# Router logits with the router weights stationary in four column groups, their partial sums copied, turned and added by one more product

## What is computed

```
h = h + merged @ w_out
xt = rms_norm(h, norm_ffn_gain)                       # 512 tokens x 1024
logits = xt.astype(f32) @ w_router.astype(f32) + b_router   # 512 x 32
top_val, top_idx = lax.top_k(logits, 4)
gates = softmax(top_val)
# each token's row goes to its 4 experts:
#   g, u = xblk @ w_up_gate[e] + b_up_gate[e];  act = swiglu(g, u);  y = act @ w_down[e] + b_down[e]
# and comes back as the sum of the 4 results, weighted with the gates
```

## Time and profile before

| | |
|---|---|
| median of 3 runs | 1762.51 us (1762.42 to 1762.52) |
| the profiled execution's own time | 1762.06 us |
| its span | 1760.2 us |
| ScalarE (ACT) busy | 1141.1 us, 65% |
| VectorE (DVE) busy | 1420.5 us, 81% |
| GpSimd (POOL) busy | 316.9 us, 18% |
| products of the logits (line 870), 64 records | 7.6 us busy |
| granted TensorE clock, mean | 0.998 |

### The profile page before, as it was taken

One profiled execution on the slowest core, in us unless ns is written; L12 is line 12 of the kernel. 1 busy time (PEld: TensorE's weight loads), 2 busy tenths in 40 slices (PEclk: granted clock), 3 DMA queues, 4 the chain that ended last, 5 costly groups with the idle time before them and its releaser, 6 DMA issues.

```text
span 1760.2 us, 26321 instructions
## 1 busy us (share of the span) xinstructions
PE 1736.3 (99%) x8957; PEld 1281.8 (73%) x8957; DVE 1420.5 (81%) x1450; ACT 1141.1 (65%) x1122; POOL 316.9 (18%) x241
## 2 busy tenths in 40 slices
PE   8999999999999999999999999999999999999997
PEld 7778777777877767777777777777777777777765
DVE  4666576567656899989888988898889888988898
ACT  4544564455454577777777777777777777777783
POOL 1102201210220111122111111121112111211153
PEclk9999999999999999999999999999999999999999
DMA  7432233133126599999999999999999999999995
GB/s 211 144 97 65 79 107 107 36 107 101 43 97 248 199 353 377 359 367 388 378 374 372 356 374 381 362 372 363 379 369 366 366 375 372 369 367 372 380 333 235
DMA packets 159059, 488.44 MB, mean 277 GB/s; under 512 B 13187, under 2 KB 83123, under 8 KB 125521
## 3 DMA queue, kind: packets, MB, share of 16 engines
q1 hardware_dynamic: 151120, 469.29, 72.6%
q0 software_dynamic: 7088, 16.52, 2.8%
q10 hardware_dynamic: 816, 2.19, 0.3%
HBM read 479.43 MB, written 24.39 MB: 286 GB/s over the span
## 4 chain that ended last, share of the span: by engine, by line
PE 96%; DVE 2%; issue 1%; ACT 0%; DMA 0%; DVEq 0%; SPq 0%; ACTq 0%
PE psum L330 28%; PE psum L332 28%; PE psum L331 28%; PE psum L987 1%; PE psum L700 1%; PE psum L730 1%; PE psum L1023 1%; PE psum L971 1%; PE psum L716 1%; PE psum L666 1%; PE psum L683 1%; DVE wL L1735 1%; PE psum L764 0%; PE psum L897 0%; PE psum L675 0%
## 5 line engine op out<-in xcount | busy, mean ns | idle before, releaser
L1735 DVE TENSOR_TENSOR wL<-wraw,wH 128x2048 fp32r<-128x2048 f32 x388 | 882.1, 2289 | 118.5 <-ACT wH L429 115.9
L429 ACT ACTIVATE wH<-wraw 128x2048 fp32r<-128x2048 f32 x388 | 744.3, 1919 | 289.5 <-PE psum L332 280.8
L330 PE MATMUL psum<-wH,xTH 128*96 128x512 f32 x1040 | 416.2, 400 | 0.5 <-DVE wL L1735 0.4
L332 PE MATMUL psum<-wH,xTL 128*96 128x512 f32 x1040 | 408.4, 393 | 0.0
L331 PE MATMUL psum<-wL,xTH 128*96 128x512 f32 x1040 | 408.2, 392 | 0.0
L330 PEld LDWEIGHTS psum<-wH,xTH 128*96 128x96 f32 x1040 | 167.9, 161 | 72.3 <-DVE wL L1735 0.8
L332 PEld LDWEIGHTS psum<-wH,xTL 128*96 128x96 f32 x1040 | 167.8, 161 | 72.4
L331 PEld LDWEIGHTS psum<-wL,xTH 128*96 128x96 f32 x1040 | 168.0, 162 | 69.3
L330 PE MATMUL psum<-wH,aTH 128*96 128x512 f32 x496 | 196.4, 396 | 0.0
L332 PE MATMUL psum<-wH,aTL 128*96 128x512 f32 x496 | 194.9, 393 | 0.0
L331 PE MATMUL psum<-wL,aTH 128*96 128x512 f32 x496 | 194.4, 392 | 0.0
(11 more groups left out here) (272 smaller groups left out, 2161.8 us busy)
## 6 DMA issues: line engine op xcount, KB each, us to landing
wraw<-in_w_up_gate SPq DMA_DIRECT2D x256, 1024.0 KB, 7.0
wraw<-in_w_down SPq DMA_DIRECT2D x128, 1024.0 KB, 7.6
fraw<-in_w_in SPq DMA_DIRECT2D x68, 512.0 KB, 4.1
yd<-in_consts SPq DMA_DIRECT2D x8, 1024.0 KB, 8.2
wraw<-yd SPq DMA_DIRECT2D x3, 2048.0 KB, 11.4
wraw<-in_w_out SPq DMA_DIRECT2D x4, 1024.0 KB, 5.2
xt<-in_x SPq DMA_DIRECT2D x4, 512.0 KB, 5.0
hres<-in_x SPq DMA_DIRECT2D x4, 512.0 KB, 5.1
```

What stands on the lines that cost most here:

```text
L330: nc.tensor.matmul(ps, lh, rh, start=start, stop=False)
L332: return nc.tensor.matmul(ps, ll, rh, start=False, stop=stop)
L429: nc.scalar.activation(wH[:, b % SPLIT, :], raw(b), ACT.Copy).then_inc(p_hi, 1)
L1735: V.tensor_tensor(wL[:, b % SPLIT, :], raw(b), wH[:, b % SPLIT, :].bitcast(F32), ALU.subtract).then_inc(p_lo, 1)
```

## The change

The router block `wr[:, k, :]` (128 x 32) becomes the stationary operand, in one of four groups of 32 columns, and the 128 tokens of `rT` move. Four partial sums, one for each k modulo 4, come out turned, in partitions 32 g to 32 g + 31 of bank 2, columns 128 to 255. ScalarE copies these 128 x 128 numbers into the new tile `lgT` (`logits_turned`), and one more product with `lgT` stationary and a constant of 128 x 32 moving (a one wherever the row modulo 32 is the column) turns and adds them (`logit_sums`). `lg_done` now counts both steps. The lists of TensorE and ScalarE are changed to place the new steps. ROWS_TURNED and LOGITS_TURNED hold the counts of `rT_ready`, which now counts the new copies too.

```
+    lgT = sb("lgT", [P, P])
...
+    ROWS_TURNED, LOGITS_TURNED = ((1, 2), (3, 4), (6, 7), (10, 11)), (5, 8, 9, 12)
...
-            def out_projection(j, q):
+            def out_projection(j, q, halves=(0, 1)):
...
-                for kk in range(2):
+                for kk in halves:
...
-                if j == NT - 1:
+                if j == NT - 1 and halves[-1] == 1:
                     last.then_inc(p_used, 1)
-                elif q == 3:
+                elif q == 3 and halves[-1] == 1:
                     last.then_inc(wo_done, 1)
...
             def logits(j):
 
-                pe.wait_ge(rT_ready, 2 * j + 2)
+                pe.wait_ge(rT_ready, ROWS_TURNED[j][1])
                 pe.wait_ge(tri_wr_ready, 2)
                 pe.wait_ge(h_ready, 4)
                 if j:
                     pe.wait_ge(top_ready, j)
                 for k in range(KD):
-                    last = nc.tensor.matmul(bank[2][:, 0:NE], rT[:, k, j * P:(j + 1) * P], wr[:, k, :],
-                                            start=k == 0, stop=k == KD - 1)
+                    g = slice(k % 4 * NE, (k % 4 + 1) * NE)
+                    last = nc.tensor.matmul(bank[2][g, P:2 * P], wr[:, k, :], rT[:, k, j * P:(j + 1) * P],
+                                            start=k < 4, stop=k >= 4, skip_group_check=True)
                 last.then_inc(lg_done, 1)
+
+            def logit_sums(j):
+
+                pe.wait_ge(rT_ready, LOGITS_TURNED[j])
+                nc.tensor.matmul(bank[2][:, 0:NE], lgT[:, :], cst[:, K_SE:K_SE + NE], start=True, stop=True).then_inc(lg_done, 1)
...
             out_projection(3, 0)
             logits(0)
             turn_rows(2)
+            logit_sums(0)
             out_projection(3, 1)
             logits(1)
             positions(0)
-            out_projection(3, 2)
+            out_projection(3, 2, (0,))
+            logit_sums(1)
+            out_projection(3, 2, (1,))
             logits(2)
             positions(1)
-            out_projection(3, 3)
+            out_projection(3, 3, (0,))
+            logit_sums(2)
+            out_projection(3, 3, (1,))
             first_rows(0)
             turn_rows(3)
             positions(2)
+            logits(3)
             first_rows(1)
-            logits(3)
+            logit_sums(3)
             first_rows(2)
...
+            def logits_turned(j):
+                act.wait_ge(lg_done, 2 * j + 1)
+                A(lgT[:, :], bank[2][:, P:2 * P], ACT.Copy).then_inc(rT_ready, 1)
+
...
             rows_turned(1)
             row_squares(2)
             row_sqrt(2)
+            logits_turned(0)
+            rows_turned(2)
             rows_out(0)
             rows_out(1)
-            rows_turned(2)
-            for b in (4, 5, 6):
-                high(act, 0, b)
+            logits_turned(1)
+            high(act, 0, 4)
+            logits_turned(2)
+            high(act, 0, 5)
+            high(act, 0, 6)
             rows_out(2)
             row_squares(3)
             act.wait_ge(p_used, 4)
             rows_turned(3)
             row_sqrt(3)
+            logits_turned(3)
...
             def route(j):
 
-                dve.wait_ge(lg_done, j + 1)
+                dve.wait_ge(lg_done, 2 * j + 2)
```

More of the change, by code:

```diff
@@ L856, in turn_rows @@
                     if j:
-                        pe.wait_ge(rT_ready, 2 * (j - 1) + half + 1)
+                        pe.wait_ge(rT_ready, ROWS_TURNED[j - 1][half])
                     for k in range(4 * half, 4 * half + 4):
@@ L982, in up_part @@
                     pe.wait_ge(b_step, BIAS_STEPS)
-                    pe.wait_ge(rT_ready, 2 * NT)
+                    pe.wait_ge(rT_ready, ROWS_TURNED[NT - 1][1])
                     pe.wait_ge(top_ready, NT)
```

## The result

Over eight runs of each, the changed kernel takes 0.42% longer: ratio 1.0042, interval 1.0033 to 1.0051. On the 1762.51 us of before that is 1769.9 us (1768.3 to 1771.5). The median of its own runs is 1771.4 us (1763.28 us for the eight runs of before beside them). Its runs do not gather around one value. They fall into two groups: two at 1765.9 and 1766.1 us, six at 1771.0 to 1772.5 us. The mean granted clock goes with them, 0.997 in the first group and 0.993 in the second. The profiled execution is one of the first group (1766.14 us, span 1764.4 us).

What follows compares the result with a forecast made beforehand. TensorE, busy 99%, was taken as the bound, with ScalarE's new order deciding: despite 3.08 us less TensorE work the stage ends 3.2 us later, so 1762.06 becomes 1765.2, plus 0.45 for the median 1765.7; range 1764.3 to 1771.0.

Steps and rivals of the forecast that it cites:

- The blocks and the sums: TensorE: a logits block takes 0.58 us plus 0.09 ahead, each sum adds 0.21; its work falls by 3.08 us.
- The chain: ScalarE's copies ahead of high 4 and 5 link three engines in one chain; route(3) starts 3.2 us later.
- The transfer: rows_out(0), issued later on ScalarE's queue, takes 2.6 to 3.9 us to land before scaled_rows(2), at no cost.
- made up: Rival: part of the delay is recovered at the first experts, leaving 0 to 2 us, 1762.5 to 1764.5; chance 0.06.
- Steps 3 and 5: TensorE waits some 2.6 us before logits(2); logits(3) then waits for rows_turned(3), and route(3) starts at 591.81 against 588.63.
- What would show it: List of signs: TensorE waiting before logits(2) and turn_rows(3), high 5 starting near 579.3, route(3) near 591.8.
- The forecast's own case: Middle stage ends 3.2 us later, 1765.7; its own bounds 1764.7 to 1766.7; chance 0.67.
- groups that do not run four at a time: Rival on TensorE's logits blocks: two at a time gives 1767.5, one at a time 1770.6; chance 0.12.
- a late transfer: Rival: rows_out(0) lands 1.6 to 2.4 us late, and low piece 4 with it, 1767.3 to 1768.2; chance 0.08.
- The chance of 0.54 for slower: Whole kernel slower by over 0.2%: 0.34 from the forecast's case and 0.20 from the slower rivals.
- one group at a time: Slow end of the column-group rival on TensorE: 1.2 us more a logits block, 4.9 in all, 1770.6.

Runs made afterwards that it cites:

- order_alone: Kernel before, with two waits added on ScalarE: high 4 waits for the second block of logits, high 5 for the third; 1769.54 us, ratio 1.0037.
- high_first: Changed kernel with ScalarE's high 4 put ahead of logits_turned(1) and high 5 ahead of logits_turned(2); 1763.26 us, ratio 1.0000.
- both_early: Changed kernel with high 4 and 5 ahead of the second and third copy, and rows_out(0), rows_out(1) right after row_sqrt(1); 1760.79 us, ratio 0.9991.
- one_group: Changed kernel with all eight products of a logits block in one group of 32 columns instead of four; 1773.79 us in a single run.
- fill_first: Changed kernel with 11 unused identity products on TensorE ahead of logits(2) alone, later pauses left open; 1771.72 us.

## Why the prediction was right in part, and where it was wrong

**The blocks and the sums: right.** Predicted 0.58 us to the next instruction and 0.09 ahead; measured 0.57 and 0.09. The Trainium skill's fourfold speedup ("TensorEngine Tiling (Array Packing)", "Theoretical Speedup") is not reached: 1.70 to 0.57 is threefold, since the first step and the change of product form cost as they do for two halves.

**The chain: right.** Predicted a pause of 2.6 us ahead of logits(2), measured 2.52; VectorE's wait for high 5 some 2 us, measured 2.02; copy 0.27, measured 0.28; a shift of 3.2 us, measured 3.2. With the pauses filled the kernel takes 1765.65 us, against the forecast of 1765.7. That number alone is in part luck: beside its own runs of before the filled kernel is 0.16% slower, 2.8 us, not 3.2. The firmer sign is the stretch from logits(0) to route(3), 24.36 us against 21.16. order_alone and high_first show that it is the order: it costs in the kernel before, and with it undone the new form costs nothing.

**The transfer: right.** Issued at 570.17, scaled_rows(2) began at 573.57, 3.4 us later, within the 2.6 to 3.9 taken. VectorE was through with it 1.01 us before high 4 let low piece 4 start.

**Nothing was made up:** 1171.6 us from route(3) to the end, before and after, in high_first and in both_early.

**The pauses themselves: wrong.** Steps 3 and 5 found the new waits of TensorE, and "What would show it" named both the one ahead of logits(2) and the one ahead of turn_rows(3), but the sum charged them at the time of standing still alone, as if every product after them ran at the clock of before, and no rival had a lower clock. In the profile of the slower group the products behind the second pause ran at 1.2 GHz and cost about 6 us more. Ten of the 14 runs of the changed kernel have that time and that mean clock (1771.0 us or more, 0.992 or 0.993), and filling the pauses removed them. That is the larger part of what was measured. The forecast's own case ended at 1766.7 us. The ratio's 1769.9 is inside the range by luck: its upper part was there for groups that do not run four at a time and for a late transfer, and neither came true. The median of the runs, 1771.4 us, is 0.4 above the top. The Trainium skill describes the effect, in "TensorE: Matmul & The Clock Gate", section "HAM oscillation": a wait between bursts of products throws the clock back to half, and the next burst starts slow. The profiles above agree, with pauses of 2.52 us, shorter than those of its example.

The trace of before could not have given the size. In it TensorE's longest pause between products is this one, and the clock behind it is 1.00:

```profile
522.03 0.47 PE L330 MATMUL psum<-wH,mTH 128*128 128x512 f32 x1 [1.58 <-DVE mTL L1743]
```

So a new pause of 2.6 us had no precedent there. The kernel's `keep_warm`, four unused products ahead of the output projection, was a hint. What decides, from run to run, after which of the pauses the clock falls was not found and is left open.

The chance of 0.54 for slower was too low because of the missing clock: the forecast's case alone stood at the edge of what can be measured, and a cost that can only add was left out of it.

**A rival's price: too low.** For one group at a time the prediction took 1.2 us a block, 4.9 in all; one_group has 1.67 - 0.37 = 1.30 a block, 5.2 in all. It changed nothing in the forecast.

## What to carry to other kernels

A copy put into an in-order engine's list stalls everything behind it; look at what stands behind it and whether the thing it waits for depends, over other engines, on that very work. Here swapping two pairs of lines was worth 3 us of chain and, in most runs, 6 us of clock. A new pause on TensorE had two prices here, the pause and the products after it at half the clock; the second depends on what hides them. Its sign was times in two groups with two mean clocks. Unused products took the second price away when all the pauses were filled; in the first pause alone they made the slow case the rule, and where they ran past their pause they held up the work behind them.

## What was not expected of the hardware

- One pause of 2.52 us on TensorE was enough for some 17 us at 1.2 GHz: in fill_first, where the pause ahead of logits(2) is filled, from 587 to 604 us; in the slower profile of the changed kernel, with 5.7 us of work between two such pauses, from 588 to 605 us. Pauses of 1.38 us (high_first, order_alone) and 1.58 us (before) left the clock at 1.00.
- The same program with the same pauses had its clock fall either after the first of them, for 3.4 us, or after the second, for some 17 us, from run to run.
- Filling the pause that came first made the slower case the rule (five of five), and filling the later ones removed it (none of ten).
- float32 products with 32 stationary and 128 moving columns run four at a time: a block of 16 records ends its starts after 0.37 us in four groups and after 1.67 in one.
